# Convolution taps on ScalarE and GpSimd, two matrix-engine channel blocks, a projection four abreast, and moved waits in the head pairs

## The chip, the core and the metric

The kernel runs on one core of a Trainium2 chip. Its engines each work through their own instruction stream and meet at semaphores: TensorE (PE, matrix products into PSUM), VectorE (DVE), ScalarE (ACT), GpSimd (POOL) and SyncE (SP, which here only issues the loads of the weights).
## The reference, cut to what matters

A sequence of 512 tokens with 1024 channels passes through two networks. The first is a gated block with two recurrent heads per pair (four pairs) and an output product; the second is a Conformer convolution layer, a feed-forward layer, banded attention and a second feed-forward layer. The change touches the head pairs and the convolution:

```python
def conformer_conv(x, w_pw1, b_pw1, w_dw, b_dw, ln_g, ln_b, w_pw2, b_pw2):
    a = jax.nn.glu(x @ w_pw1 + b_pw1, axis=-1)
    y = lax.conv_general_dilated(          # depthwise: 31 taps for each channel, causal
        a, w_dw[:, None, :], window_strides=(1,), padding=((30, 0),),
        dimension_numbers=('NWC', 'WIO', 'NWC'), feature_group_count=1024) + b_dw
    y = jax.nn.silu(layernorm(y, ln_g, ln_b))
    return y @ w_pw2 + b_pw2
```

So `y[t, c]` is a sum over k = 0..30 of `w_dw[k, c] * a[t - 30 + k, c]`, then a norm over the channels of each token, then a 1024 x 1024 product.

## The kernel before

**Layout.** Channels lie on the 128 partitions in 8 blocks (KC = 8), tokens along the free axis (512). A weight matrix comes as chunks of 128 output channels. A chunk n uses slot j = n % 4 in four tiles: SP loads it into `w_raw`, ScalarE rounds it into `w_hi` (`w_high`, called ahead of use as `ahead`: `ahead` of chunk n casts chunk n + 3), GpSimd subtracts to get the rest `w_lo` (`w_low`), and only then may SP load chunk n + 4 into `w_raw`. `dense` makes a chunk's product in PSUM (`gps`, slot j) from 3 x 8 matmuls of 128 x 512: high by high, high by low, low by high, for each of 8 input blocks k. It waits for `lo_ready` (the weights) and `evicted` (the PSUM slot read out), and sets `tile_done`.

**Head pairs** (`pair`, run four times, 20 chunks each). TensorE's program is: chunks 0 to 3, the token-major chunks 4 and 5 (`dense_tokens`), chunks 6 and 7, `hgrn_levels(0)` (28 small matmuls), the token-major chunks 10 and 11, `hgrn_rest(0)`, chunk 12, scores, chunk 13, scores, `attend(0, 0)`, and so on. ScalarE copies the chunks 6 and 7 out of PSUM (`rqk`, and in four pieces with the rows exchanged `unit`) and casts the weights in between. VectorE's `decayed` (18 products and 3 scalings, most with two operands in SBUF) makes the operands of `hgrn_levels`; `near_levels` and `near_eye` collect near scores for `attend`, `causal` those of the retention heads.

**Convolution.** While TensorE makes the 16 chunks of the first pointwise product (pw1), VectorE turns two chunks into one block of the gated input `glu` and fills its time with taps: `scalar_tensor_tensor` from `glu` into a PSUM bank of `aps`, two blocks abreast. It makes the 31 taps of the blocks 0 to 4 (155). The blocks 5, 6 and 7 are TensorE's (PE_CONV = 3): for each tap a 128 x 128 diagonal matrix in a high and a low part, made by ScalarE (`diagonals`, 62 for a block), is multiplied with the shifted `glu_hi` and `glu_lo` (3 matmuls a tap, 93 a block). ScalarE copies the sums out (`conv_out`). GpSimd adds up the blocks 0 to 6 of `conv` in `total` (`hbuf[3]`); two matmuls with ones give the mean (`mean_done`). Then VectorE centres, ScalarE squares, TensorE adds the squares over the channels, ScalarE makes the reciprocal root, VectorE and ScalarE build the operands `xa_hi` and `xa_lo` of the second pointwise product (pw2).

**pw2.** Its chunk 0 is made by `dense_behind`, in which 2 matmuls follow on each block of `xa_hi` as it comes and the 8 with `xa_lo` stand at the end; the chunks 1 to 7 follow by `dense`. `residual` reads each chunk out of PSUM into `res` (VectorE), builds the next operand and the squares (ScalarE), and casts the next weights.

Every engine's order is written out by hand, so the order below is the order of the program.

## Time and profile before

| | us |
|---|---|
| median of 3 runs | 1752.26 (1751.93 to 1752.62) |
| the profiled execution, device time | 1750.22 |
| its span | 1748.4 |
| TensorE busy in the span | 1671.2 (96%) |
| VectorE, ScalarE, GpSimd busy | 809.3, 766.7, 672.1 |
| mean granted TensorE clock | 0.983 |

The busy share of TensorE includes the modelled end of each matmul, so a stretch that reads as full can still run at half the clock; the granted clock and the count of matmuls in a stretch tell that. Times of rows count from the span's start.

### The profile page before, as it was taken

Reading aid. Unit: us, or ns where it says so; the run is one execution under the profiler, and the core shown is the slowest. Engines: PE = TensorE matmul, PEld = TensorE weight load, DVE = VectorE, ACT = ScalarE, POOL = GpSimd, SP = SyncE. Lnnn points to the kernel's source line nnn. Section 1 sums busy time; section 2 is a strip of 40 time slices with the busy share of each in tenths; the row PEclk is TensorE's granted clock in tenths of the full one; section 3 lists DMA queues with packets and bytes.
Section 4 is the critical chain, followed back from the end, with each engine's and each line's share of the span. In section 5 each row is a group of like instructions: output and inputs, shape, how many; then the busy total and the mean of one; then the engine's idle time right before and its main releaser. Section 6 shows DMA issues by size and latency. Waiting matters only on the chain.

```text
span 1748.4 us, 22097 instructions
## 1 busy us (share of the span) xinstructions
PE 1671.2 (96%) x8005; PEld 1360.0 (78%) x8005; DVE 809.3 (46%) x1391; ACT 766.7 (44%) x1179; POOL 672.1 (38%) x281
## 2 busy tenths in 40 slices
PE   4899999999999999998999999999999999999997
PEld 2777877877877778875888888888887888888885
DVE  6864564564565539994322122126465321121123
ACT  4544554553553664646443222226476442222222
POOL 3343343343343434312444444445223444344342
PEclk7999999999999999998999999999999999999999
DMA  9321331331331446201223223223211333222231
GB/s 373 103 91 57 103 105 60 101 102 50 107 98 58 134 70 183 96 1 44 90 95 103 89 96 101 92 96 120 73 49 60 98 96 96 96 96 96 96 96 61
DMA packets 49876, 167.59 MB, mean 96 GB/s; under 512 B 4987, under 2 KB 9500, under 8 KB 49308
## 3 DMA queue, kind: packets, MB, share of 16 engines
q1 hardware_dynamic: 43696, 154.50, 26.6%
q10 hardware_dynamic: 6124, 12.33, 3.0%
q8 instruction: 38, 0.62, 0.2%
q14 instruction: 18, 0.15, 0.0%
HBM read 161.56 MB, written 5.24 MB: 95 GB/s over the span
## 4 chain that ended last, share of the span: by engine, by line
PE 83%; DVE 8%; ACT 4%; issue 3%; POOL 1%; DMA 0%; ACTq 0%; DVEq 0%; POOLq 0%
PE gps L1379 23%; PE gps L1381 23%; PE gps L1380 22%; POOL w_lo L431 1%; DVE ada_w L910 1%; PE gps L1408 1%; PE gps L1630 1%; PE gps L1632 1%; PE gps L1631 1%; PE gps L1409 1%; PE gps L1410 1%; PE aps L1548 1%; PE aps L1682 1%; DVE at_near L1005 1%; DVE gates L1125 1%
## 5 line engine op out<-in xcount | busy, mean ns | idle before, releaser
L431 POOL TENSOR_TENSOR w_lo<-w_raw,w_hi 128x1024 fp32r<-128x1024 f32 x260 | 644.8, 2483 | 980.6 <-ACT w_hi L495 980.6
L1379 PE MATMUL gps<-xa_hi,w_hi 128*128 128x512 f32 x1152 | 460.3, 400 | 21.2 <-POOL xa_lo L438 13.3
L1381 PE MATMUL gps<-xa_hi,w_lo 128*128 128x512 f32 x1152 | 450.5, 391 | 0.0
L1380 PE MATMUL gps<-xa_lo,w_hi 128*128 128x512 f32 x1152 | 450.3, 391 | 0.0
L495 ACT CAST w_hi<-w_raw 128x1024 fp32r<-128x1024 f32 x260 | 270.9, 1045 | 154.4 <-PE gps L1381 137.0
L1379 PE MATMUL gps<-xb_hi,w_hi 128*128 128x512 f32 x736 | 291.6, 396 | 2.4 <-issue 1.2
L1381 PE MATMUL gps<-xb_hi,w_lo 128*128 128x512 f32 x736 | 288.9, 393 | 0.0
L1380 PE MATMUL gps<-xb_lo,w_hi 128*128 128x512 f32 x736 | 286.3, 389 | 0.0
L1379 PEld LDWEIGHTS gps<-xa_hi,w_hi 128*128 128x128 f32 x1152 | 217.5, 189 | 74.9 <-issue 18.5
L1380 PEld LDWEIGHTS gps<-xa_lo,w_hi 128*128 128x128 f32 x1152 | 217.7, 189 | 46.2 <-issue 3.1
L1381 PEld LDWEIGHTS gps<-xa_hi,w_lo 128*128 128x128 f32 x1152 | 217.3, 189 | 46.0
L1379 PEld LDWEIGHTS gps<-xb_hi,w_hi 128*128 128x128 f32 x736 | 138.4, 188 | 33.0 <-issue 3.6
L1381 PEld LDWEIGHTS gps<-xb_hi,w_lo 128*128 128x128 f32 x736 | 138.2, 188 | 32.0
L1380 PEld LDWEIGHTS gps<-xb_lo,w_hi 128*128 128x128 f32 x736 | 138.2, 188 | 31.1 <-issue 0.5
L1284 DVE TENSOR_TENSOR hbuf<-gps,rstd 128x512 f32<-128x512 f32 x44 | 30.4, 692 | 202.1 <-PE gps L1381 202.1
L1227 DVE SCALAR_TENSOR_TENSOR aps<-glu,vec,aps 128x512 f32<-128x512 f32 x145 | 99.6, 756 | 1.0
L1408 PE MATMUL gps<-w_hi,xa_hi 128*128 128x256 f32 x256 | 75.4, 295 | 14.5 <-POOL w_lo L431 14.5
L1296 DVE TENSOR_TENSOR res<-gps,res 128x512 f32 x32 | 22.1, 692 | 143.8 <-PE gps L1381 143.8
L1283 DVE TENSOR_TENSOR sq<-gps,rstd 128x512 f32<-128x512 f32 x44 | 30.4, 692 | 121.4 <-PE gps L1381 106.2
L782 ACT ACTIVATE sq<-sq 128x512 f32<-128x512 f32 x44 | 27.9, 634 | 118.4 <-DVE sq L1283 118.4
L1409 PE MATMUL gps<-w_hi,xa_lo 128*128 128x256 f32 x256 | 74.9, 293 | 0.0
L1410 PE MATMUL gps<-w_lo,xa_hi 128*128 128x256 f32 x256 | 74.8, 292 | 0.0
(252 smaller groups left out, 1955.0 us busy)
## 6 DMA issues: line engine op xcount, KB each, us to landing
w_raw<-weights_dram SPq DMA_DIRECT2D x268, 512.0 KB, 3.3
ada_w<-ada_in_dram SPq DMA_DIRECT2D x8, 1024.0 KB, 15.8
gates<-ret_tab_dram ACTq DMA_DIRECT2D x4, 1024.0 KB, 5.8
rel_scratch_dram<-rel_rows ACTq DMA_DIRECT2D x1, 3072.0 KB, 34.5
x<-x_turned_dram SPq DMA_DIRECT2D x2, 1024.0 KB, 9.7
res<-xT_dram ACTq DMA_DIRECT2D x1, 2048.0 KB, 8.8
bias<-rel_scratch_dram ACTq DMA_DIRECT2D x1, 2048.0 KB, 8.5
outT_dram<-y SPq DMA_DIRECT2D x8, 256.0 KB, 2.2
```

What stands on the lines that cost most here:

```text
L431: TT(w_lo[:, j, :], w_raw[:, j, :], w_hi[:, j, :].bitcast(F32), ALU.subtract).then_inc(lo_ready[j], 1)
L495: nc.scalar.copy(w_hi[:, j, :], w_raw[:, j, :]).then_inc(hi_ready[j], 1)
L782: nc.scalar.activation(sq[:, m, :], sq[:, m, :], ACT.Silu).then_inc(silu_ready, 1)
L1227: made_at[c] = own.mark(STT(bank, src, w, bank, ALU.mult, ALU.add))
L1283: TT(sq[:, m, :], full(I, 2 * m), rstd[:], ALU.mult).then_inc(evicted[2 * m], 1)
L1284: TT(h, full(I, 2 * m + 1), rstd[:], ALU.mult).then_inc(evicted[2 * m + 1], 1)
L1379: mm(gps[:, j, :], w_hi[:, j, w], x[0][:, k, :], start=k == 0, stop=False)
L1380: mm(gps[:, j, :], w_hi[:, j, w], x[1][:, k, :], start=False, stop=False)
L1381: last = mm(gps[:, j, :], w_lo[:, j, w], x[0][:, k, :], start=False, stop=k == blocks - 1)
L1408: mm(out, x[0][:, k, tok], wh, start=k == 0, stop=False)
L1409: mm(out, x[1][:, k, tok], wh, start=False, stop=False)
L1410: last = mm(out, x[0][:, k, tok], wl, start=False, stop=k == KC - 1)
```

## The change

In words:

- **Taps.** VectorE makes the blocks 0, 2 (its taps 0 to 19 only), 3, 4 and 5: 144 taps, three blocks abreast at the end, in three banks of `aps`, by the plan of `tap_schedule`. Block 1 and the taps 20 to 30 of block 2 (42 in all) are made by ScalarE as products into five buffers (the first of them straight into `conv`) and added into `conv` by GpSimd (41 adds, each waiting for the one before it). TensorE makes only the blocks 6 and 7.
- **Mean.** GpSimd adds only the blocks 0 and 1; the others enter the mean by six matmuls with ones, three within the last block's taps, four with the last one behind them.
- **Diagonals.** Those of the second TensorE block are made one by one, with three products after every fourth.
- **pw2.** `dense_abreast` makes the chunks 0 to 3 together: for each block k of `xa_hi` 8 matmuls (two for each chunk), then the parts with `xa_lo` chunk by chunk. The cast of chunk 3 is moved ahead. The eight `normed_residual` of VectorE move from before the mean to behind the centring (four) and behind the building of the operands (four). The reciprocal root stands in `lnv`.
- **Pairs.** For the chunks 6 and 7 ScalarE casts the next weights first, frees the PSUM slot after one copy, and makes `unit` from `rqk` in SBUF. TensorE makes k = 6, 7 of chunk 13 behind the scores of the retention heads. VectorE runs `near_eye(1)` ahead of a product and a gate.

The new schedule and the core of the diff:

```python
def tap_schedule():
    stop = {c: SHARED_AT if c == SHARED_CHUNK else TAPS for c in DVE_CHUNKS}
    ...
            c = min(bank, key=lambda c: last[c])
            run.append((c, done[c], bank[c], done[c] == stop[c] - 1))
            done[c] += 1
            last[c] = n
            n += 1
            if done[c] == stop[c]:
                free.append(bank.pop(c))
                order.append(c)
```

```diff
-DVE_CONV = 5
-PE_CONV = KC - DVE_CONV
-TAP_RUNS = (8, 11, 12, 12, 12, 12, 12)
+DVE_CHUNKS = (0, 2, 3, 4, 5)
+POOL_CHUNK = 1
+SHARED_CHUNK = 2
+SHARED_AT = 20
+PE_FIRST = 6
+PE_CONV = KC - PE_FIRST
+POOL_TAPS_FROM = 10
+TAP_BANKS = (0, 2, 3)
+TAP_RUNS = (8, 10, 12, 12, 12, 12, 12)
...
             pool.wait_ge(both_ready, 1)
+            for n in range(3, 2 * KC):
+                w_low(START["pw1"] + n // SLOTS, n % SLOTS)
+                if n >= POOL_TAPS_FROM:
+                    taps(2 * (n - POOL_TAPS_FROM), 2 * (n - POOL_TAPS_FROM) + 2)
             low(0)
...
+                c, k = POOL_TAPS[i]
+                pool.wait_ge(product, i + 1)
+                if i > 1:
+                    pool.wait_ge(tap_added, i - 1)
...
+                TT(conv[:, c, :], conv[:, c, :], products[(i - 1) % len(products)], ALU.add).then_inc(tap_added, 1)
...
+                        if i > len(products):
+                            act.wait_ge(tap_added, i - len(products))
+                        nc.scalar.mul(products[(i - 1) % len(products)], src, w).then_inc(product, 1)
...
                     b = full(at(6 + n), 2 + n)
-                    nc.scalar.copy(rqk[:, n, :], b)
+                    ahead(at(7 + n), (7 + n) % SLOTS)
+                    nc.scalar.copy(rqk[:, n, :], b).then_inc(evicted[2 + n], 1)
+                    act.wait_ge(evicted[2 + n], at(6 + n) + 2)
                     for r in range(0, P, ROT_HALF):
                         o = r ^ ROT_HALF
-                        last = nc.scalar.copy(unit[o:o + ROT_HALF, n, :], b[r:r + ROT_HALF, :])
-                    last.then_inc(evicted[2 + n], 1)
-                    ahead(at(7 + n), (7 + n) % SLOTS)
+                        last = nc.scalar.copy(unit[o:o + ROT_HALF, n, :], rqk[r:r + ROT_HALF, n, :])
+                    last.then_inc(turn_ready, 1)
...
+            for k in range(TAPS):
+                diagonal(1, k)
+                if k % 4 == 3:
+                    tap_products(at, at + 3)
+                    at += 3
+                if k == 3 * TAP_GROUP - 1:
+                    conv_out(0)
+            tap_products(at, len(POOL_TAPS))
...
-                feature(13)
+                feature(13, 0, 6)
                 ret_scores(2)
                 ret_scores(3)
+                feature(13, 6)
                 attend(0, 0)
...
                 was_evicted(16)
+                near_eye(1)
                 take_norm(0, 1)
                 z_gate(17, 1, 1, "ret_norm_g")
-                near_eye(1)
...
-            for c in range(KC):
-                normed_residual(c)
...
+            for c in range(KC // 2):
+                normed_residual(c)
             dve.wait_ge(center_done, KC)
             dve.wait_ge(x_ready, KC * X_PW2)
             x_build(conv, lambda c: vcol("ln_g", c), xa_hi, xa_lo)
+            for c in range(KC // 2, KC):
+                normed_residual(c)
...
+            for c in TAPS_END[-2:]:
+                pe.wait_ge(conv_done, TAPS_END.index(c) + 1)
+                add_to_mean(conv[:, c, :])
+            pe.wait_ge(tap_added, len(POOL_TAPS) - 1)
+            add_to_mean(conv[:, SHARED_CHUNK, :])
             pe.wait_ge(conv_copied, PE_CONV)
-            mm(aps[:, 1, :], ones[:], conv[:, KC - 1, :], start=False, stop=True).then_inc(mean_done, 1)
+            add_to_mean(conv[:, KC - 1, :], last=True).then_inc(mean_done, 1)
...
+            def dense_abreast(I, x, high, low):
...
+                for k in range(KC):
+                    high(k)
+                    w = slice(k * P, (k + 1) * P)
+                    for j in range(SLOTS):
+                        mm(gps[:, j, :], w_hi[:, j, w], x[0][:, k, :], start=k == 0, stop=False)
+                        mm(gps[:, j, :], w_lo[:, j, w], x[0][:, k, :], start=False, stop=False)
+                for j in range(SLOTS):
+                    for k in range(KC):
...
+                        last = mm(gps[:, j, :], w_hi[:, j, k * P:(k + 1) * P], x[1][:, k, :], start=False, stop=k == KC - 1)
+                    last.then_inc(tile_done[j], 1)
```

GpSimd, from the last weight parts of pw1 to pw2; before (`hbuf<-hbuf,conv` are the sums of blocks):

```order
L431 TENSOR_TENSOR w_lo<-w_raw,w_hi 128x1024 x4
L462 REGISTER_ALU
L462 COMPARE_AND_BRANCH
L457 TENSOR_TENSOR glu_lo<-glu,glu_hi 128x542
L431 TENSOR_TENSOR w_lo<-w_raw,w_hi 128x1024 x2
L457 TENSOR_TENSOR glu_lo<-glu,glu_hi 128x542
L431 TENSOR_TENSOR w_lo<-w_raw,w_hi 128x1024
L457 TENSOR_TENSOR glu_lo<-glu,glu_hi 128x542
L480 TENSOR_TENSOR hbuf<-conv 128x512
L480 TENSOR_TENSOR hbuf<-hbuf,conv 128x512 x5
L431 TENSOR_TENSOR w_lo<-w_raw,w_hi 128x1024
```

and GpSimd after the change, in the second half of the same place (`conv<-conv,hbuf` and `conv<-conv,sq` are the adds of products):

```order
L497 TENSOR_TENSOR glu_lo<-glu,glu_hi 128x542
L471 TENSOR_TENSOR w_lo<-w_raw,w_hi 128x1024
...
L471 TENSOR_TENSOR w_lo<-w_raw,w_hi 128x1024
L508 TENSOR_TENSOR conv<-conv,sq 128x512 x2
L508 TENSOR_TENSOR conv<-conv,hbuf 128x512 x3
L508 TENSOR_TENSOR conv<-conv,sq 128x512 x2
L531 TENSOR_TENSOR hbuf<-conv 128x512
L508 TENSOR_TENSOR conv<-conv,hbuf 128x512 x3
...
L471 TENSOR_TENSOR w_lo<-w_raw,w_hi 128x1024 x2
```

Five sums of blocks are gone, 41 adds of products stand between the weight parts, and the last two weight parts of pw2's first four stand behind the last add.

TensorE, from the end of the convolution into pw2; before:

```order
L1632 MATMUL gps<-glu_hi,diag_lo 128x512
L1636 MATMUL aps<-hbuf,ones 128x512
L1638 MATMUL aps<-conv,ones 128x512
L1417 MATMUL aps<-sq,ones 128x512 x8
L1391 MATMUL gps<-xa_hi,w_hi 128x512
L1392 MATMUL gps<-xa_hi,w_lo 128x512
```

and TensorE at the same place after the change, from the last block's 25th tap:

```order
L1732 MATMUL gps<-glu_hi,turn_lo 128x512
L1720 MATMUL aps<-hbuf,ones 128x512
L1720 MATMUL aps<-conv,ones 128x512 x2
L1730 MATMUL gps<-glu_hi,turn_hi 128x512
...
L1732 MATMUL gps<-glu_hi,turn_lo 128x512
L1720 MATMUL aps<-conv,ones 128x512 x4
L1513 MATMUL aps<-sq,ones 128x512 x8
L1485 MATMUL gps<-xa_hi,w_hi 128x512
L1486 MATMUL gps<-xa_hi,w_lo 128x512
```

Three matmuls of the mean stand within the taps and four behind them; before there were two, both behind.

ScalarE in a pair, at the chunks 6 and 7 (`w_hi` are the casts of the chunks 10, 11 and 12); before:

```order
L616 COPY val<-gps 128x2x256 x2
L623 COPY rqk<-gps 128x512
L626 COPY unit<-gps 32x512 x4
L493 ISA
L495 CAST w_hi<-w_raw 128x1024
L623 COPY rqk<-gps 128x512
```

and ScalarE there after the change:

```order
L669 COPY val<-gps 128x2x256 x2
L546 ISA
L548 CAST w_hi<-w_raw 128x1024
L677 COPY rqk<-gps 128x512
L681 COPY unit<-rqk 32x512 x4
L548 CAST w_hi<-w_raw 128x1024
```

Each cast stands ahead of its chunk's copies.

## Rows read from the trace of the kernel before

**Rows 1.** The page's part 1: busy time, share of the span, instructions of each engine.

```profile
PE 1671.2 (96%) x8005; PEld 1360.0 (78%) x8005; DVE 809.3 (46%) x1391; ACT 766.7 (44%) x1179; POOL 672.1 (38%) x281
```

**Rows 2.** TensorE's waits over the span: waiter, releaser, total us, times, longest.

```profile
PE gps L1408 <- POOL w_lo L431: 14.5, 4, 3.6
...
PE gps L1391 <- ACT xa_hi L768: 5.5, 1, 5.5
...
PE aps L1548 <- DVE at_near L1018: 3.1, 3, 1.1
PE aps L1536 <- DVE at_r L1032: 2.4, 4, 0.6
```

**Rows 3.** Stretches: engines' busy us (instructions), granted clock, DMA share, GB/s.

```profile
646.00:718.00 72.00, 71.70 (x312) 58.63 (x313) 63.36 (x96) 35.81 (x78) 34.98 (x16) 1.00 0.69 169
718.00:783.00 65.00, 65.00 (x280) 52.52 (x279) 64.11 (x90) 39.63 (x129) 13.39 (x9) 1.00 0.05 16
783.00:799.70 16.70, 9.85 (x22) 2.98 (x20) 7.34 (x13) 12.30 (x17) 0.00 (x0) 1.00 0.00 0
799.70:811.60 11.90, 11.80 (x25) 6.27 (x26) 8.34 (x13) 10.85 (x16) 0.95 (x1) 0.57 0.00 1
811.60:855.20 43.60, 43.60 (x194) 36.04 (x193) 14.90 (x22) 16.61 (x23) 18.26 (x8) 1.00 0.29 97
```

**Rows 4.** A tap's third matmul: duration ns min/median/max, first and last start.

```profile
L1632 PE MATMUL gps<-glu_hi,diag_lo x62: 387/396/404, 718.5 to 782.8; 128*128 128x512 f32 x62
```

**Rows 5.** The chain that ended last, at the mean: start, us, what.

```profile
783.24 0.86 PE aps L1636 x2
```

**Rows 6.** VectorE in order of time, taps to centring: start, us, instruction [idle before].

```profile
721.58 23.80 DVE L1227 SCALAR_TENSOR_TENSOR aps<-glu,vec,aps 128x512 f32<-128x512 f32 x36
...
756.73 17.38 DVE L1227 SCALAR_TENSOR_TENSOR aps<-glu,vec,aps 128x512 f32<-128x512 f32 x22
...
785.18 4.88 DVE L1266 SCALAR_TENSOR_TENSOR conv<-aps,conv 128x512 f32<-128x512 f32 x8 [1.85 <-PE aps L1638]
```

**Rows 7.** GpSimd in order of time, from 711 to 779 us.

```profile
711.56 4.80 POOL L431 TENSOR_TENSOR w_lo<-w_raw,w_hi 128x1024 fp32r<-128x1024 f32 x2
...
742.47 1.30 POOL L480 TENSOR_TENSOR hbuf<-conv 128x512 f32<-128x512 f32 x1
...
774.97 1.74 POOL L480 TENSOR_TENSOR hbuf<-hbuf,conv 128x512 f32<-128x512 f32 x1 [16.77 <-DVE conv L1229]
776.86 1.56 POOL L480 TENSOR_TENSOR hbuf<-hbuf,conv 128x512 f32<-128x512 f32 x1
```

**Rows 8.** GpSimd's slowest 128 x 512 subtractions, line 438.

```profile
L438 POOL TENSOR_TENSOR xa_lo<-hbuf,xa_hi x6: 1279/2110/2260, 28.2 to 48.9; 128x512 fp32r<-128x512 f32 x6
```

**Rows 9.** ScalarE: a 128 x 512 product with a column of `vec`.

```profile
817.89 0.73 ACT L524 ACTIVATE xb_hi<-res,vec 128x512 fp32r<-128x512 f32 x1 [3.26 <-DVE res L1184]
```

**Rows 10.** A pair, in order of time: VectorE, ScalarE, GpSimd, and two later meetings.

```profile
219.82 2.51 DVE L982 TENSOR_TENSOR packed<-packed,q 128x256 f32<-128x256 f32 x7 [1.01 <-ACT hbuf L569]
...
223.52 1.06 ACT L495 CAST w_hi<-w_raw 128x1024 fp32r<-128x1024 f32 x1
...
224.66 3.38 POOL L431 TENSOR_TENSOR w_lo<-w_raw,w_hi 128x1024 fp32r<-128x1024 f32 x1 [15.95 <-ACT w_hi L495]
...
225.86 2.26 DVE L994 TENSOR_SCALAR q_far<-q_far,hbuf 128x128 f32<-128x128 f32 x1
...
228.75 4.71 POOL L431 TENSOR_TENSOR w_lo<-w_raw,w_hi 128x1024 fp32r<-128x1024 f32 x2 [0.71 <-ACT w_hi L495]
...
263.67 5.10 POOL L431 TENSOR_TENSOR w_lo<-w_raw,w_hi 128x1024 fp32r<-128x1024 f32 x1 [5.55 <-ACT w_hi L495]
...
864.93 5.23 POOL L431 TENSOR_TENSOR w_lo<-w_raw,w_hi 128x1024 fp32r<-128x1024 f32 x2 [0.47 <-ACT w_hi L495]
```

**Rows 11.** Stretches of the first and third pair, columns as in rows 3.

```profile
96.60:103.40 6.80, 5.57 (x26) 5.60 (x27) 5.54 (x10) 0.00 (x0) 3.29 (x2) 0.50 0.58 199
...
362.80:366.20 3.40, 3.40 (x18) 3.40 (x18) 2.72 (x4) 0.00 (x0) 1.60 (x1) 0.50 0.68 190
```

More of the change, by code:

```diff
@@ L53 @@
 ADA_CHUNKS = 2 * KC
-DVE_CONV = 5
-PE_CONV = KC - DVE_CONV
-TAP_RUNS = (8, 11, 12, 12, 12, 12, 12)
+DVE_CHUNKS = (0, 2, 3, 4, 5)
[5 more added lines that the diff above has]
+POOL_TAPS_FROM = 10
+POOL_TAPS = [(POOL_CHUNK, k) for k in range(TAPS)] + [(SHARED_CHUNK, k) for k in range(SHARED_AT, TAPS)]
+TAP_BANKS = (0, 2, 3)
+TAP_RUNS = (8, 10, 12, 12, 12, 12, 12)
+def tap_schedule():
+    stop = {c: SHARED_AT if c == SHARED_CHUNK else TAPS for c in DVE_CHUNKS}
+    done, bank, last, order, runs, n = {c: 0 for c in DVE_CHUNKS}, {}, {}, [], [], 0
+    free = list(TAP_BANKS)
+    for upto in range(1, KC + 1):
+        left = sum(stop[c] - done[c] for c in DVE_CHUNKS)
+        run = []
+        for _ in range(TAP_RUNS[upto - 1] if upto < KC else left):
+            new = [c for c in DVE_CHUNKS if c < upto and c not in bank and c not in order]
+            if new and free:
+                bank[new[0]] = free.pop(0)
+                last[new[0]] = -1
+            c = min(bank, key=lambda c: last[c])
[6 more added lines that the diff above has]
+                order.append(c)
+        runs.append(run)
+    return runs, order
+TAP_PLAN, TAPS_END = tap_schedule()
 TAP_GROUP = 8
 TAP_GROUPS = -(-TAPS // TAP_GROUP)
-XB_PAD = 240
+XB_PAD = 224
 PAIR_CHUNKS = 20
@@ L257, in program @@
         dve_own = sem("dve_own")
+        product = sem("product")
+        tap_added = sem("tap_added")
         consts_in = sem("consts_in")
@@ L460, in _, with taps @@
+            def taps(first, last):
+                for i in range(max(first, 1), last):
+                    tap(i)
             pool.wait_ge(both_ready, 1)
-            w_low(START["pw1"], 3)
-            with pool.Fori(START["pw1"] + 1, START["pw2"]) as i:
-                for j in range(SLOTS):
-                    w_low(i, j)
+            for n in range(3, 2 * KC):
+                w_low(START["pw1"] + n // SLOTS, n % SLOTS)
+                if n >= POOL_TAPS_FROM:
+                    taps(2 * (n - POOL_TAPS_FROM), 2 * (n - POOL_TAPS_FROM) + 2)
@@ L465, in _ @@
             low(0)
+            at = 2 * (2 * KC - POOL_TAPS_FROM)
+            taps(at, at + 6)
+            low(1)
             w_low(START["pw2"], 0)
+            taps(at + 6, at + 12)
             w_low(START["pw2"], 1)
-            low(1)
-            w_low(START["pw2"], 2)
-            low(2)
-            total = hbuf[:, 3, :]
-            for n, c in enumerate(range(1, KC - 1)):
-                if c < DVE_CONV:
-                    pool.wait_ge(conv_done, c + 1)
-                else:
-                    pool.wait_ge(conv_copied, c - DVE_CONV + 1)
-                if n > 0:
-                    pool.wait_ge(conv_sum, n)
-                TT(total, conv[:, 0, :] if n == 0 else total, conv[:, c, :], ALU.add).then_inc(conv_sum, 1)
+            taps(at + 12, TAPS)
@@ L481, in _ @@
+            total = hbuf[:, 3, :]
+            pool.wait_ge(tap_added, TAPS - 1)
+            pool.wait_ge(conv_done, TAPS_END.index(DVE_CHUNKS[0]) + 1)
+            TT(total, conv[:, DVE_CHUNKS[0], :], conv[:, POOL_CHUNK, :], ALU.add).then_inc(conv_sum, 1)
+            taps(TAPS, len(POOL_TAPS))
+            w_low(START["pw2"], 2)
             w_low(START["pw2"], 3)
@@ L1209, in normed_residual, with taps @@
                 STT(res[:, c, :], res[:, c, :], vcol("final_g", c), rstd[:], ALU.mult, ALU.mult).then_inc(res_ready, 1)
[L1211 to L1236 removed]
+            made_at = {}
+            def taps(plan):
+                for c, k, b, last in plan:
+                    src, w, bank = glu[:, c, k:k + T], vcol("w_dw", c + k * KC), aps[:, b, :]
+                    if k == 0:
+                        dve.wait_ge(evicted[2 * (c % 2)], START["pw1"] + c // 2 + 2)
+                        before = [n for n, d in enumerate(TAPS_END) if bank_of[d] == b and n < TAPS_END.index(c)]
+                        if before:
+                            dve.wait_ge(conv_done, before[-1] + 1)
+                        made_at[c] = own.mark(TS(bank, src, w, vcol("b_dw", c), ALU.mult, ALU.add))
+                    else:
+                        own.wait(made_at[c])
+                        if not last:
+                            made_at[c] = own.mark(STT(bank, src, w, bank, ALU.mult, ALU.add))
+                        else:
+                            STT(conv[:, c, :], src, w, bank, ALU.mult, ALU.add).then_inc(conv_done, 1)
+            bank_of = {c: b for run in TAP_PLAN for c, _, b, _ in run}
             def halves_in(c):
@@ L1620, in _, with add_to_mean @@
             layer_then("pw1", KC // 2, xb, x_wait(X_CONV_IN), lambda: sum_running(RMS_FIRST, double=True))
+            def add_to_mean(src, first=False, last=False):
+                return mm(aps[:, 1, :], ones[:], src, start=first, stop=last)
             for m in range(PE_CONV):
```

116 lines of the change are left out of this document (61 added, 55 removed).

## The prediction

> **What bounds the kernel.** First the busy shares: TensorE is busy for 96% of the span, every other engine for under half [rows 1]. Then its waits, which name the places where it is not: 14.5 us for GpSimd's `w_lo` in the four pairs, 5.5 at pw2, 3.1 and 2.4 in the pairs behind `near_eye` and `causal` [rows 2]. Then the stretches, with clock and counts of matmuls [rows 3]. From 646 to 783 us TensorE is full: pw1, then the taps. From 783 to 799.7 only the norm's chain runs. From 799.7 to 811.6 TensorE reads as full, but makes 25 matmuls in 11.9 us, at a mean clock of 0.57, where the next stretch makes 194 in 43.6. So what counts is TensorE's own work and the few places where it is fed too slowly. A matmul of 128 x 512 costs 43.6 / 192 = 0.227 us (8 chunks of 24), one of the taps (782.8 - 718.5) / 276 = 0.233 (the third matmul of the first and of the last of 93 taps) [rows 4].
>
> **Taps, TensorE's side.** 93 matmuls go: 93 x 0.233 = 21.7 us. The taps end at 718.0 + 186 x 0.233 = 761.3 instead of 783.0. Against that the mean grows from two ones-matmuls to seven, each 0.86 [rows 5]. Three of them stand within the taps: 764.0, plus about 0.5 for the last group of diagonals (below): 764.5.
>
> **Taps, VectorE's side.** 144 taps instead of 155. Of these 78 lie in pw1's gaps (79 before), which TensorE bounds. 66 are left from about 721.1 (one tap less stands ahead of 721.58). Two blocks abreast cost 23.80 / 36 = 0.661 a tap, one alone 17.38 / 22 = 0.79 [rows 6]. By the plan only the last 7 stand alone: 59 x 0.661 + 7 x 0.79 = 44.5, so the last `conv_done` comes at 765.6. VectorE had ended its taps at 774.9 (756.73 + 17.38 and one more) and then run `normed_residual` under TensorE's last block; both leave the path.
>
> **Taps, GpSimd's side.** An add of 128 x 512 took 1.30 alone; chained ones start 0.15 behind the end of the one before (774.97 + 1.74 = 776.71, next at 776.86) [rows 7]. So a step costs 1.45. In pw1, for each 10.9 us of TensorE (two chunks), GpSimd gets 4 adds and 2 `w_lo` of 2.40: 10.6 us. That fits, since the weights run some 5 us ahead. `low(0)` waits for ScalarE's cast behind pw1's chunk 14, which ends one chunk (5.4) ahead of the taps' start at 717.9, at 712.5; with cast, copy and subtraction (2.8) it ends at 715.3, 2.7 ahead of the taps. From there: one `glu_lo` (1.15), two `w_lo` (4.8), 30 adds and the sum of two blocks: 715.3 + 5.95 + 31 x 1.45 = 766.2. This is a tie with VectorE's 765.6. VectorE's taps read PSUM and one SBUF operand, and they kept 0.661 under the add at 742.47, which took 1.30; so I charge neither for the other. The step is the least certain term: 1.30 is its lower bound; above it stand 776.86 - 774.97 = 1.89, beside VectorE's two-operand `normed_residual`, and the slowest subtraction of this size, 2.26 [rows 8], again beside VectorE work with two SBUF operands. I take 1.45, since the adds beside taps ran alone.
>
> **ScalarE.** It was busy for 39.6 of 65 us in the taps' stretch, 124 of its 129 instructions diagonals [rows 3]. 62 of those go (18 us) and 24 products at most 0.73 each come [rows 9]: still under 45 of 49 us. But a product waits for the add five places back. The last three ahead of diagonal 28 need add 33, which is 23 steps behind 715.3 + 5.95, at 754.6; a product and six diagonals of 0.29 later, at 757.0, the group stands, and TensorE wants them at 756.5. That is the 0.5 above.
>
> **The mean.** TensorE ends at 764.5, block 5 comes at 765.6, its ones-matmul to 766.5, block 2 (add 41 at 766.2) to 767.4, block 7 to 768.3. Centring starts at 768.4 instead of 785.18 [rows 6]. **Gain 16.7 us.** The chain behind it is unchanged (four `normed_residual`, 2.6 us, fit into VectorE's wait for the root; the other four end before chunk 0 of pw2 does).
>
> **pw2.** Chunk 0 takes 11.9 us where 24 x 0.227 = 5.4 would do: 6.4 lost. `xa_hi` comes every 1.2 us, with 2 matmuls behind it; now 8, which is 1.8 us at the high clock. So feeding stops being a limit and only the clock is left. Mean 0.57 over 11.9 us means some 10.2 us at half clock [rows 3]. In the pairs, where matmuls followed back to back, a low stretch lasted 3.4 us in two of them and 6.8 in the first [rows 11]. Bounds 0 and 10.2; I take 5, nearer to rows 11 since TensorE will be as full there; it costs 2.6. Chunk 4 must wait for a read-out, a cast and a `w_lo` behind chunk 0: with chunk 0 ending 5.5 us before the four are done, 0.7 + 1.2 + 1.05 + 2.4 leaves 0.2 to wait. **Gain 6.4 - 2.8 = 3.6 us** (1 to 6).
>
> **Pairs.** (a) The 3.6 us wait for chunk 11's weights. Chunk 10's cast moves from 223.5 to 220.6 and chunk 11's from 227.6 to 224.7. But GpSimd's `w_lo` of chunk 10, free to start at 224.66, took 3.38 instead of 2.4, and at 263.67 another took 5.10: both times VectorE was in the row of 18 products of `decayed` (0.35 each for the first 14, two SBUF operands each). The first time the row went from 219.82 to 225.8; the scaling behind it then took 2.26, and GpSimd's `w_lo` ended with it at 228.04, 2.3 behind the row [rows 10]. GpSimd gets in only when the row ends. With the cast at 220.6 the row has begun, so `w_lo` of chunk 10 still ends at 228.0. Only chunk 11's moves: from 228.75 to about 228.3 (one or two of VectorE's instructions go between, as at 864.93, where two took 5.23). Gain 0.4 (bounds 0 and 2.9, rival 2; a loss only if VectorE's delay reached TensorE). VectorE then stands up to 2.4 longer before `near_levels(0)`, and with it the rotation of `rqk`; TensorE wants those only behind chunk 12, after the token chunks (12 us) and a chunk of 5.4.
> The Trainium skill (SBUF — State Buffer, "Who interferes with whom") has this as a rule: a VectorE instruction with two SBUF inputs and a GpSimd one that reads SBUF share a port pair that is held for the whole instruction. By that rule the moved cast brings little, which the 5.10 us bear out; without it the gain would be the rival's.
> (b) The 0.6 wait behind `causal`: six matmuls now stand over it, 1.4 us. Gain 0.6. (c) The 1.0 wait for `near_eye(1)`: two VectorE instructions (0.7 each) go from ahead of it. Gain 1.0. Both moved gates are wanted later than that. Four pairs: **gain 4 x 2.0 = 8.0 us.** The low stretches of the pairs (6.8, 3.4 and 3.4 us) [rows 11] I leave as they are.
>
> **Sum.** 16.7 + 3.6 + 8.0 = 28.3 us. The profiled execution goes from 1750.2 to 1721.9; the median lies 2.0 above it before, so 1752.3 - 28.3 = **1724.0 us**.
>
> **Rivals.**
> 1. GpSimd sets the end of the taps. For it: the tie above, 41 chained steps. Against: adds beside taps took 1.30. It decides from a step of 1.46. At 1.70 its last add comes at 773.9 and the mean 7.3 later: 1731.3. Chance 0.12.
> 2. `w_lo` of chunk 10 slips between VectorE's products. For it: nothing in the rows. Against: the 5.10 us. Then chunk 11's weights are there at 228.2, 2.9 us earlier than before, 2.5 more a pair; and the shorter idle may keep the clock up (13.6 us low, 6.8 lost). 1724 - 10 - 6.8 = 1707. Chance 0.08.
> 3. **Slower.** GpSimd's steps cost what its slowest subtractions did: 2.26 [rows 8] plus 0.15 = 2.41. Then the 11 adds in pw1 come 10.6 late (4.9 of it free), the 31 behind them 29.8: last add at 801.7, mean at 803.9, 18.7 later than before, against 11.6 gained elsewhere: 1752.3 + 7.1 = 1759. It decides from a step of 2.24. Against: those rows ran beside VectorE's two-operand work, the taps are not that. Chance 0.03.
> 4. The change does not do what it says at pw2 and in the pairs: TensorE stays at half clock for 10 us, the reordered waits come back elsewhere. Only the taps pay: 1752.3 - 16.7 - 1.5 = 1734. Chance 0.12.
>
> **Numbers.** The forecast has the rest, 0.65, with its own range 1718 to 1729. The range of 8 in 10 takes in rivals 1 and most of 4: 1712 to 1734. A run can tell about 0.2% (3.5 us) from no change: faster by more 0.95, within 0.02, slower 0.03.
>
> **What would show it.** TensorE's taps x186, ending at 761 of the old times (some 8 us less by the pairs' gain). Seven ones-matmuls of 0.86. The last VectorE tap and the last GpSimd add within 1 us of each other, about 44.5 and 51 us behind the last gate and `low(0)`. GpSimd's add at 1.30 with 0.15 between. Centring 16.7 earlier against pw1's end. Pairs: TensorE's wait for `w_lo` at 3.2 instead of 3.6 each, the 0.6 and 1.0 gone; GpSimd's first `w_lo` stretched to some 6 us. pw2: 96 matmuls in about 25 us, a low clock stretch of 3 to 7 us. I am wrong if GpSimd's adds take over 1.5 a step, if a new wait for `diag_ready` or a product shows on TensorE, or if the pairs change by more than 3 us each.

## The result and the profile after the change

| | before | after |
|---|---|---|
| median | 1752.11 us (4 runs, 1751.93 to 1752.62) | 1710.89 us (4 runs, 1709.66 to 1713.00) |
| profiled execution, its span | 1750.22, 1748.4 | 1709.66, 1707.9 |
| mean granted TensorE clock | 0.983 (profiled execution) | 0.984 to 0.989 (all four runs) |

The ratio is 0.9766, with a 95% interval of 0.9749 to 0.9782. Of all the runs below one was slow, 7962 us of a run of e4, and no median takes it in. The forecast of 1724.0 was 13.1 us too high, and the measured time lies 1.1 us below its range. Its direction was right, and so was its largest term. Stage by stage, from the same marks in both traces:

| stage | before | after | gain | forecast |
|---|---|---|---|---|
| start to the first cast of pw1 (mostly the pairs) | 642.66 | 626.65 | 16.0 | 8.0 |
| to the first squares of the norm (pw1, taps, mean) | 143.9 | 127.55 | 16.4 | 16.7 |
| norm and pw2 | 68.6 | 64.3 | 4.3 | 3.6 |
| the rest, whose code is unchanged | 893.2 | 889.4 | 3.8 | 0 |
| sum | | | 40.5 | 28.3 |

So two stages hold nearly the whole error of these two executions, 12.2 us: the pairs, and a part of the kernel whose code the change does not touch.

**The convolution came nearly as forecast.** VectorE, GpSimd and TensorE of the kernel after, at the end of the taps (start, us, instruction; these answer to [rows 6] and [rows 7]):

```profile
705.53 29.05 DVE L1309 SCALAR_TENSOR_TENSOR aps<-glu,vec,aps 128x512 f32<-128x512 f32 x44
...
744.38 4.70 DVE L1309 SCALAR_TENSOR_TENSOR aps<-glu,vec,aps 128x512 f32<-128x512 f32 x6
744.84 2.72 POOL L508 TENSOR_TENSOR conv<-conv,sq 128x512 f32<-128x512 f32 x2
...
747.71 1.27 POOL L508 TENSOR_TENSOR conv<-conv,hbuf 128x512 f32<-128x512 f32 x1
...
749.11 0.75 DVE L1311 SCALAR_TENSOR_TENSOR conv<-glu,vec,aps 128x512 f32<-128x512 f32 x1
...
749.91 2.84 PE L1720 MATMUL aps<-conv,ones 128*128 128x512 f32 x6 [1.18 <-DVE conv L1311]
```

A VectorE tap takes 29.05 / 44 = 0.660 (forecast 0.661). Two adds of GpSimd take 2.72, and a chained one costs 1.43 (1.45). VectorE's last tap ends at 749.86, GpSimd's last add at 748.98: the tie. A ones-matmul leaves two rows in these views (`x6` above are three of them, `x2` in [rows 5] is one), so each costs 0.86, as forecast.

**The waits of TensorE** in the kernel after (waiter, releaser, total us, times, longest), against [rows 2]:

```profile
PE gps L1504 <- POOL w_lo L471: 5.8, 4, 2.8
PE gps L1485 <- ACT xa_hi L851: 5.5, 1, 5.5
...
PE aps L1572 <- DVE packed L1068: 3.7, 6, 0.7
...
PE aps L1720 <- DVE conv L1311: 1.2, 1, 1.2
```

The wait for `w_lo` fell from 14.5 to 5.8, not to the forecast 12.8. Those for `at_near` and `at_r` are gone. One for `packed` is new.

**The pairs went in two ways.** Second pair and third pair of the kernel after, in order of time (the place of [rows 10]):

```profile
215.14 2.51 DVE L1065 TENSOR_TENSOR packed<-packed,q 128x256 f32<-128x256 f32 x7 [1.02 <-ACT hbuf L622]
...
216.99 11.03 POOL L471 TENSOR_TENSOR w_lo<-w_raw,w_hi 128x1024 fp32r<-128x1024 f32 x3 [12.96 <-ACT w_hi L548]
...
221.19 2.27 DVE L1077 TENSOR_SCALAR q_far<-q_far,hbuf 128x128 f32<-128x128 f32 x1
...
225.93 0.35 PE L1504 MATMUL gps<-w_hi,xa_hi 128*128 128x256 f32 x1 [2.85 <-POOL w_lo L471]
...
343.40 4.72 DVE L1065 TENSOR_TENSOR packed<-packed,q 128x256 f32<-128x256 f32 x7 [1.02 <-ACT hbuf L622]
345.26 2.51 POOL L471 TENSOR_TENSOR w_lo<-w_raw,w_hi 128x1024 fp32r<-128x1024 f32 x1 [12.97 <-ACT w_hi L548]
...
348.94 1.15 PE L1572 MATMUL aps<-packed 128*128 128x128 f32 x8 [0.73 <-DVE packed L1068]
```

In the second pair VectorE's row of products is undisturbed (2.51) and GpSimd waits: its three `w_lo` take 11.03 instead of some 7.2, and the first alone 6.38 instead of 2.5. In the third GpSimd gets in between two products, its `w_lo` takes 2.51, and VectorE's row takes 4.72. Both times GpSimd asks 1.85 us behind the row's start. The forecast knew the first way only. For TensorE both ways come to the same: it starts chunk 10 28.5 us behind chunk 4 in either (29.3 before).

**The low-clock stretches of the pairs are gone** in this execution: those of [rows 11] and one more, 13.6 us together. **pw2** has 3.4 us of low clock instead of 10.2. After the change, from the first to the last of the four abreast, then the rest (columns as in [rows 3]):

```profile
764.70:785.00 20.30, 17.64 (x71) 14.49 (x72) 13.12 (x20) 12.38 (x18) 0.00 (x0) 0.92 0.01 1
785.00:818.50 33.50, 33.35 (x147) 27.31 (x146) 21.56 (x22) 16.46 (x23) 18.42 (x7) 1.00 0.33 110
```

**The unchanged code got faster.** Stretches of 84 us in the feed-forward layer, TensorE full at clock 1.00; before:

```profile
856.00:940.00 84.00, 84.00 (x367) 68.60 (x366) 22.36 (x30) 37.84 (x42) 39.00 (x16) 1.00 0.29 94
```

and after:

```profile
820.00:904.00 84.00, 84.00 (x372) 69.50 (x371) 23.09 (x31) 38.30 (x43) 38.73 (x16) 1.00 0.30 99
```

367 matmuls against 372 (the records have gaps of a few, so the spacing of neighbours is the better measure: 228.9 ns against 226.7). The slower ones read `xb_hi` or `xb_lo`; those that read `xa` start every 226.7 to 226.9 ns in both kernels. The one edit that moves `xb` is `XB_PAD = 224` instead of 240: it is the size, in floats for each partition, of an unused tile ahead of `xb`. It is in the diff, and neither the words on the change nor the prediction mention it.

### The profile page after: what moved, and what is told of

Same layout as the page of the kernel before. It is cut to its first block, busy times and chain, and to the rows that moved or that the text cites. A ratio compares the mean times of both kernels' runs of the same rounds, so it can differ in the third digit from the quotient of the medians.

```text
span 1707.9 us, 21958 instructions
## 1 busy us (share of the span) xinstructions
PE 1640.8 (96%) x7922; PEld 1339.2 (78%) x7922; DVE 821.4 (48%) x1380; ACT 773.1 (45%) x1157; POOL 734.0 (43%) x316
## 4 chain that ended last, share of the span: by engine, by line
PE 79%; DVE 11%; ACT 3%; issue 3%; POOL 2%; DMA 1%; ACTq 0%; DVEq 0%; POOLq 0%; SPq 0%
PE gps L1458 22%; PE gps L1460 22%; PE gps L1459 22%; DVE aps L1309 4%; POOL w_lo L471 2%; DVE ada_w L993 1%; PE gps L1504 1%; PE gps L1506 1%; PE gps L1505 1%; DMA w_raw<-weights_dram 1%; PE aps L1644 1%; PE aps L1792 1%; PE aps L1572 1%; PE aps L1650 1%; PE aps L1802 1%
## 5 line engine op out<-in xcount | busy, mean ns | idle before, releaser
L471 POOL TENSOR_TENSOR w_lo<-w_raw,w_hi 128x1024 fp32r<-128x1024 f32 x260 | 662.4, 2551 | 923.8 <-ACT w_hi L548 923.7
L1458 PE MATMUL gps<-xa_hi,w_hi 128*128 128x512 f32 x1128 | 452.2, 401 | 21.0 <-POOL xa_lo L478 13.0
L1460 PE MATMUL gps<-xa_hi,w_lo 128*128 128x512 f32 x1128 | 441.5, 391 | 0.0
L1459 PE MATMUL gps<-xa_lo,w_hi 128*128 128x512 f32 x1128 | 441.5, 391 | 0.0
L1458 PEld LDWEIGHTS gps<-xa_hi,w_hi 128*128 128x128 f32 x1128 | 213.2, 189 | 74.3 <-issue 18.8
L1459 PEld LDWEIGHTS gps<-xa_lo,w_hi 128*128 128x128 f32 x1128 | 213.5, 189 | 45.0 <-issue 3.1
L1460 PEld LDWEIGHTS gps<-xa_hi,w_lo 128*128 128x128 f32 x1128 | 213.1, 189 | 45.4
L1309 DVE SCALAR_TENSOR_TENSOR aps<-glu,vec,aps 128x512 f32<-128x512 f32 x134 | 91.5, 745 | 0.7
```

The lines of the kernel that those rows point to most:

```text
L471: TT(w_lo[:, j, :], w_raw[:, j, :], w_hi[:, j, :].bitcast(F32), ALU.subtract).then_inc(lo_ready[j], 1)
L1309: made_at[c] = own.mark(STT(bank, src, w, bank, ALU.mult, ALU.add))
L1458: mm(gps[:, j, :], w_hi[:, j, w], x[0][:, k, :], start=k == 0, stop=False)
L1459: mm(gps[:, j, :], w_hi[:, j, w], x[1][:, k, :], start=False, stop=False)
L1460: last = mm(gps[:, j, :], w_lo[:, j, w], x[0][:, k, :], start=False, stop=k == blocks - 1)
```

## The experiments

All times are medians. The changed kernel itself is 1710.9, and 1711.6 when run again beside some of these (e5); the kernel before is 1750.5 to 1752.1, by chip. A run's low-clock stretches move it by 1 to 3 us, so differences under 2 us are read from the traces, not from the medians.

### The place of xb: 240, 224 and others

```diff
-XB_PAD = 224
+XB_PAD = 240
```

> The changed kernel with XB_PAD back at 240, so xb_hi and xb_lo lie 64 bytes further on, nothing else. In the stretches whose code the change leaves alone, matmuls that read xb started every 226.7 ns after the change and every 228.9 ns before it; those that read xa 226.7 in both. Theory (placement): the 2.2 ns come from where xb lies. Then all 2208 xb matmuls (3 x 736) start every 228.9 ns again, and the time rises by 2208 x 2.2 ns = 4.9 us, to about 1715.8. Rival (something else in the change, or the state of the chip in that execution): 226.7 ns stays and the time stays within 1.5 us of 1710.9.

Measured 1716.5 (1714.4 to 1719.1), 5.2 above the mean of the changed kernel's two medians. The spacing is 229 ns again.

> The kernel before with XB_PAD = 224 and nothing else. Placement: its xb matmuls start every 226.7 ns, the time falls by 4.9 us, from 1752.1 to 1747.2. Rival: 228.9 ns and 1752 stay. If placement is right, both this and the run on the changed kernel must move, by the same 4.9 with opposite signs.

Measured 1746.7, ratio 0.9977 (0.9966 to 0.9987), 4.3 faster; spacing 226.7. **Both directions moved by about what 2208 matmuls at 2.2 ns give, 4.9.** The traces say it without the noise of the low stretches. From the first matmul with `xb_hi` behind pw2 to the end the kernel before takes 898.9 us and the changed one with 240 takes 898.5; all 14 profiled executions with 224, that of e2 among them, take 894.9 to 895.4. pw1 takes 93.1 with 240 and 92.4 to 92.5 with 224. Placement is shown as the cause. The pad also moves every tile behind `xb`, `glu` among them; but matmuls that read `xa` and the taps, which read `glu`, keep their spacing, so it is the place of `xb` that counts. What about it counts took four more runs, each with another number in the same line:

> The changed kernel with XB_PAD = 232: xb_hi and xb_lo lie 32 bytes further on than at 224 and 32 short of 240. At 224 their matmuls start every 226.7 ns, at 240 mostly every 228.9. If any distance from the good place costs the same: 228.9 ns, 1715.8. If the cost grows with the distance: more or less than that. If only the place at 240 is bad: 226.7 ns, 1711.

> The changed kernel with XB_PAD = 192: xb lies 128 bytes ahead of its place at 224. By the allocation its byte address in a partition is 118912 at 224, a multiple of 128, 64 past one at 240 (228.x ns) and 32 past one at 232 (229 to 233 ns, 13 us slower). If the 128-byte alignment counts: 226.7 ns and 1711. If the place itself counts (distance to w_hi or another tile): another spacing, more than 228 ns.

> The changed kernel with XB_PAD = 160, so xb lies 256 bytes ahead of its good place (byte 118656 of a partition). The good place, 118912, differs from the places of w_hi, w_lo and xa_hi (32896, 49280, 65664) by multiples of 2048; those at +64, +32 and -128 bytes do not and were slow. If what counts is a distance to these tiles that is a multiple of 256, this one is good: 226.7 ns, 1711. If only a larger multiple counts, it is slow like 192: 229 to 233 ns, 1723 to 1726.

> The changed kernel with XB_PAD = 96, 512 bytes ahead of the good place. Multiple of 512 (or of 256): 226.7 ns, 1711. If only 1024 or 2048 counts: slow, 1716 to 1726.

| pad | bytes from the place at 224 | spacing in the feed-forward layer, ns | median, us |
|---|---|---|---|
| 240 | +64 | 228.9 | 1716.5 |
| 232 | +32 | 233.3 | 1723.9 |
| 192 | -128 | 232.4 to 233.3 | 1725.6 (2 runs) |
| 160 | -256 | 226.7 to 226.8 | 1712.6 (2 runs) |
| 96 | -512 | 226.7 to 226.8 | 1713.2 (2 runs) |

From the first matmul with `xb_hi` behind pw2 to the end it takes 906.7 us at pad 232, 906.0 at 192, and 895.0 at 160 and at 96. One row of each, TensorE's groups by line in a stretch of 84 us of the feed-forward layer (out<-in, count, busy us, mean ns; the mean is the length of one row, which goes with the spacing but is not the spacing); pad 232:

```profile
L1459 PE MATMUL gps<-xb_lo,w_hi 128*128 128x512 f32 x106 | 41.9, 395 | 0.0
```

and pad 160:

```profile
L1459 PE MATMUL gps<-xb_lo,w_hi 128*128 128x512 f32 x118 | 45.9, 389 | 0.0
```

Alignment to 128 bytes, which I took for the rule after e12, fell with pad 192. Places that lie a multiple of 256 bytes from the tiles of the weights and of `xa` were good, the three others bad. Whether it is the distance to the weights or the byte address itself (all good ones leave 128 when divided by 256), no run tells apart.

### The pairs' edits, together and one by one

> The changed kernel with the three edits of the head pairs undone (the casts and copies of chunks 6 and 7, chunk 13 in one piece, near_eye behind the gate). Theory: the edits give 4 x 2.3 = 9.3 us by the shorter waits, and a further 6.8 us because the long wait for the w_lo of chunk 11 (3.6 us, now 1.0 to 2.8) was what made the clock fall: low-clock stretches come back behind that wait in two or three of the pairs. Time 1710.9 + 16 = 1727. Rival: the waits come back but the low stretches were only this kernel's luck in one execution: 1720. Forecast's own number for the edits was 8.0: 1719.

The three edits taken back: 1725.8 (1725.3 to 1726.2), 14 to 15 more. TensorE's waits in this run:

```profile
PE gps L1503 <- POOL w_lo L471: 14.4, 4, 3.6
...
PE aps L1643 <- DVE at_near L1100: 3.0, 3, 1.0
PE aps L1631 <- DVE at_r L1114: 2.4, 4, 0.6
```

A pair lasts 132.4, with a low stretch of 3.4 us in three of the four. The low stretches came back with the waits.

> The changed kernel as it is, as the measure for the three runs beside it. Expected 1710.9 (1709.5 to 1713). In its profile: a pair in which GpSimd's first w_lo gets in between VectorE's products (w_lo 2.5 us, the row of products 4.7 instead of 2.5) has no low-clock stretch behind it; one in which it does not (w_lo 4.2, TensorE's wait for w_lo 2.8 instead of 1.0) has one of 3.4 us. So far 7 of 7 and 4 of 5 pairs went that way.

Measured 1711.6 (1709.2 to 1717.2). The one pair in which GpSimd did not get in had no low stretch this time, and its first `w_lo` took 6.38, not 4.2.

```diff
-                    ahead(at(7 + n), (7 + n) % SLOTS)
-                    nc.scalar.copy(rqk[:, n, :], b).then_inc(evicted[2 + n], 1)
-                    act.wait_ge(evicted[2 + n], at(6 + n) + 2)
+                    nc.scalar.copy(rqk[:, n, :], b)
...
-                        last = nc.scalar.copy(unit[o:o + ROT_HALF, n, :], rqk[r:r + ROT_HALF, n, :])
-                    last.then_inc(turn_ready, 1)
+                        last = nc.scalar.copy(unit[o:o + ROT_HALF, n, :], b[r:r + ROT_HALF, :])
+                    last.then_inc(evicted[2 + n], 1)
+                    ahead(at(7 + n), (7 + n) % SLOTS)
```

> The changed kernel with the casts of the chunks 10 and 11 behind the copies again (rqk and unit both from PSUM), the other two pair edits kept. Forecast's number for this edit: 0.4 a pair, 1.6 us in all: 1712.5. Present theory: TensorE's wait for w_lo is 3.6 in every pair again instead of 1.0 or 2.8, less the 1.2 us that it now waits for packed: 1.0 a pair (4 us), and the longer wait lets the clock fall in all four pairs, 3.4 us of it each (1.7 us of time): 1710.9 + 4 + 4 = 1719.

Measured 1721.3 (1719.9 to 1721.6): 9.7 for an edit forecast at 1.6. The pairs last 130.6, 130.3 and 131.6, where the changed kernel has 128.2. Less 1.6 for each 3.4 us of low clock (below) that is 129.0, 128.7 and 128.4: **the waits alone are worth some 0.5 a pair, near the forecast (0.4); the rest is the clock**, low in all four pairs. The 0.5 is a lower bound: two of these low stretches began while TensorE still stood, and cost less than 1.6 for each 3.4. Read at the start of chunk 10, ahead of the low stretches, the edit is worth 0.8 to 0.9 (29.3 against 28.5 behind chunk 4).

```diff
-                feature(13, 0, 6)
+                feature(13)
                 ret_scores(2)
                 ret_scores(3)
-                feature(13, 6)
```

> The changed kernel with chunk 13 in one piece ahead of the retention scores. Forecast: the 0.6 us wait for at_r comes back in each pair, 2.4 us: 1713.3. Rival: the scores then come earlier and something behind them (attend, the gates) is late by as much, so nothing changes: 1711.

Measured 1716.3, 4.7 more. Its undisturbed pairs last 128.8, so 0.6 a pair is the edit, as forecast. The one with a low stretch lasts 130.4: 1.6 for 3.4 us of low clock. That stretch (columns as in [rows 3]):

```profile
226.90:230.20 3.30, 3.30 (x18) 3.30 (x17) 2.83 (x5) 0.00 (x0) 1.16 (x1) 0.51 0.76 228
```

> The changed kernel with VectorE's near_eye(1) behind the product and the gate of chunk 17. Forecast: TensorE waits 1.0 us for at_near in each pair again, 4 us: 1714.9. The trace before had that wait three times, 3.1 us: 1714.0. Rival: nothing, 1711.

Measured 1718.2, 6.6 more. Its undisturbed pairs last 129.6 and 129.5: 1.3 for the edit (forecast 1.0). The wait for `at_near` is back at 3.1 in all.

So the waits are worth (0.5 to 0.9) + 0.6 + 1.3 = 2.4 to 2.8 a pair against 2.0 forecast; all three together 2.7 (the one pair of the kernel before without a low stretch lasts 130.9, those of the changed kernel 128.2).

### What lets the clock fall

All profiled executions but those of e9 and e13, which change TensorE's order there, can be counted together: 18 executions, 72 pairs, sorted by TensorE's longest idle time between chunk 7 and chunk 10, and by whether the clock was low in the 18 us that begin 2 us behind the start of chunk 10's `w_lo`:

| longest idle, us | pairs | with a low stretch |
|---|---|---|
| up to 1.0 (GpSimd got in among the first seven products only) | 33 | 0 |
| 2.65 to 2.9 | 23 | 18 |
| 3.6 (the old order of casts) | 16 | 13 |

The expectations of e9 quote an earlier count with 15 of 16 for the last row; it is 13. So not every long idle time was followed by a low clock, but no short one was. In the 13 executions with the changed order of casts and nothing that forces it, GpSimd failed to get in in 20 of 52 pairs, though it always asked 1.85 us behind the row's start. Nine of the 20 executions also have a low stretch of 3.4 us behind the pairs, between 563 and 590 us; what brings it is open.

```diff
                         TT(q_part, q_part, right(qe, level), ALU.mult)
+                    if e == 0:
+                        dve.wait_ge(lo_ready[2], at(10) + 2)
                     for level in range(LEVELS):
```

> The changed kernel in which VectorE waits, between the 7 products with q and the 7 with key of decayed(0), until w_lo of chunk 10 is made. So GpSimd always gets in (in the changed kernel it did in about 3 pairs of 4) and TensorE's wait for w_lo should be 1.0 in all four pairs. If the length of that idle time is what lets the clock fall: no low-clock stretch in any pair, mean clock at the upper end of the changed kernel's runs (0.988 or more in every run), 1710, with a narrower spread. If the low stretches are chance, they come in one pair of four as before and 1711.5 stays.

Measured 1715.7, 4 slower, low stretches in two pairs. The expectation missed. VectorE waits, and then the next `w_lo` gets in among the second seven products:

```profile
220.49 4.65 DVE L1070 TENSOR_TENSOR packed<-packed,key 128x256 f32<-128x256 f32 x7 [2.30 <-POOL w_lo L471]
...
221.71 2.41 POOL L471 TENSOR_TENSOR w_lo<-w_raw,w_hi 128x1024 fp32r<-128x1024 f32 x1 [1.26 <-ACT w_hi L548]
...
225.19 4.12 PE L1574 MATMUL aps<-packed 128*128 128x128 f32 x20 [2.65 <-DVE packed L1070]
```

TensorE is idle for 2.65 in one piece, now for `packed`, and the clock falls: nearly the same length, another cause of the wait. The same came by itself in the third pair of e1, with a low stretch too. That speaks for the idle time as such. An order in which GpSimd gets in every time, and only once, was not found.

### Taking the wait away altogether

```diff
+                for low in range(2):
                     for t in range(NT):
...
+                            if low:
+                                last = mm(out, x[0][:, k, tok], wl, ...)
+                            else:
+                                mm(out, x[0][:, k, tok], wh, ...)
+                                mm(out, x[1][:, k, tok], wh, ...)
```

> The changed kernel with another order in dense_tokens (chunks 4, 5 and 10, 11 of a pair, and two chunks later on): first the 64 matmuls with w_hi, which wait only for the casts, then the 32 with w_lo. The w_lo then has some 7 us more. Theory: the idle time of TensorE in front of these chunks (1.0 to 2.8 us a pair, 5.8 in all) goes, and with it every low-clock stretch behind it, since these came behind 15 of 16 waits of 3.6 us, 5 of 7 of 2.8 and 0 of 16 of 1.0: no low stretch in any pair. 1711.2 - 5.8 - about 1.5 = 1704. Rival (the clock does not follow this wait): only 5.8 goes, low stretches in one pair in four stay: 1705.5, with low stretches in the pairs. Rival (the weights are late anyway): the wait moves to chunk 12: 1711.

Measured 1735.7 (1732.5 to 1736.6): 24 slower, against every theory. First pair, VectorE, GpSimd and TensorE:

```profile
109.96 5.14 POOL L471 TENSOR_TENSOR w_lo<-w_raw,w_hi 128x1024 fp32r<-128x1024 f32 x2 [10.23 <-ACT w_hi L548]
110.25 2.63 DVE L1054 TENSOR_TENSOR packed<-cum 128x256 f32<-128x256 f32 x1
112.80 2.58 DVE L1055 TENSOR_TENSOR packed<-cum 128x256 f32<-128x256 f32 x1
...
119.38 0.71 DVE L1101 COPY_PREDICATED at_near<-eye_mask,aps 128x512 f32<-128x512 int32 x1
...
120.14 3.35 PE L1616 MATMUL aps<-rqk 64*128 64x512 f32 x6 [5.20 <-DVE at_near L1101]
```

The wait for `w_lo` is gone, and TensorE comes sooner to the scores. But the casts come sooner too, so two `w_lo` fall into VectorE's subtractions of `exponents(1)` and hold up two of them (2.6 each where the others take 0.41). `near_eye(0)` behind them is 4.4 late, TensorE stands for 5.2, and each pair has 6.8 to 10.2 us of low clock:

```profile
118.80:128.80 10.00, 8.66 (x19) 5.51 (x20) 4.45 (x10) 7.98 (x7) 3.61 (x2) 0.51 0.04 9
```

In the changed kernel `near_eye(0)` ends 0.9 to 1.2 us before TensorE's scores begin. That was all the room there was.

```diff
-                dve.wait_ge(rot_ready, p * 2 + 2)
-                exponents(1)
                 near_eye(0)
+                dve.wait_ge(rot_ready, p * 2 + 2)
+                exponents(1)
```

> The changed kernel with the order of e9 in dense_tokens (parts with w_lo last) and VectorE's near_eye(0) ahead of exponents(1) instead of behind it. In e9 TensorE waited up to 5.2 us a pair for near_eye(0), which stood behind 14 products of exponents(1), and the clock then fell for 6.8 to 10.2 us in each pair. Theory: with the 14 products out of its way near_eye(0) is done 5 us ahead of its need, so neither wait is left, no low-clock stretch comes in a pair, and the gain looked for in e9 appears: 1711.2 - 5.8 - 1.5 = 1704. Rival: VectorE is simply the longer chain of a pair once TensorE's waits are gone; the wait then moves to at_r or packed and the time stays above 1711.

Measured 1711.6, but in two groups: 1708.6, 1708.7, 1708.8 and 1714.4 against 1726.9 and 1727.0. The undisturbed pairs last 127.8. In the profiled execution one pair lasted 133.4: there GpSimd got into `exponents(1)` and TensorE waited 3.1 for `at_r`. Neither theory: three runs gain 2 to 3 us, and two lose 15 to 16. Neither of these two was profiled, so what made them slower is not shown. No version beat the changed kernel in its median.

> The changed kernel with near_eye(0) ahead of exponents(1) and nothing else. In the changed kernel near_eye(0) ends 1.8 us before TensorE's scores begin, so it is covered: no change, 1711, within 2 us. If it is faster by more, a hidden wait hung on it; if it is slower, ScalarE's decays(1) (which wait for exponents(1), now 0.6 later) are tight.

Measured 1718.5 (1712.4 to 1724.2), 7 slower instead of equal. In one pair VectorE waits 2.42 for `near_eye(0)`'s input; `exponents(1)` then starts later and meets the two `w_lo`, and TensorE waits 4.2 for `at_r`. The 1.8 us of the expectation were 0.9 to 1.2, and they were room at the place where `near_eye(0)` stood, not at the place to which I moved it.

### pw2, and who ends the taps

```diff
-            dense_abreast(START["pw2"], xa, ...)
-            layer("pw2", xa, first=SLOTS)
+            dense_behind(START["pw2"], 0, xa, ...)
+            layer("pw2", xa, first=1)
```

> The changed kernel with pw2's chunk 0 made alone again as the operand comes (dense_behind) and chunks 1 to 7 after it, everything else as changed. Theory: four abreast is worth the 4.3 us that the stage became shorter, most of it by a low-clock stretch of 3.4 instead of 10.2 us: time 1715.2, with a low stretch of about 10 us at chunk 0. Rival: the shorter low stretch came from the shorter idle before it (the mean) and not from the order: the stretch stays at 3.4 us and the time rises by only 6.4 - 3.4/2 - 2.8 lost in feeding, 1 to 2 us, to 1712.5.

Measured 1715.8 (1713.6 to 1717.4), 4 to 5 more; the low stretch is 13.7 us. From the first squares to the first matmul with `xb_hi` it takes 63.9, in the changed kernel 58.7, before 63.0. The idle time before it was the same (5.5), so the shorter low stretch comes from the order. In all 17 profiled executions with the four abreast it was 3.4 or 6.8 us, in the three others 10.2 or 13.7.

```diff
-SHARED_AT = 20
+SHARED_AT = 24
```

At 24 ScalarE's loop over the products is also bounded by their number, which is 38 then.

> The changed kernel with block 2 shared at tap 24 instead of 20: VectorE makes 4 taps more (0.66 each), GpSimd 4 adds fewer (1.43 each). In the changed kernel VectorE's last tap ends at 749.9 and GpSimd's last add at 749.0. If VectorE sets the end: centring starts 4 x 0.66 = 2.6 us later, 1713.8. If GpSimd sets it (first rival of the forecast): up to 5.7 us earlier, bounded by TensorE's own end at 747.7, so 1 to 2 us faster.

```profile
PE aps L1720 <- DVE conv L1311: 4.8, 1, 4.8
```

> The changed kernel with block 2 shared at tap 16: VectorE 4 taps fewer, GpSimd 4 adds more, ScalarE 4 products more. If the two really tie, GpSimd now ends 4 x 1.43 = 5.7 later, at 754.7, and sets the end: centring 4.8 us later, 1716. Together with the run at 24: if both are slower by their own engine's step, the forecast's tie is shown. If the step of GpSimd grows beside VectorE (forecast's 1.89 or 2.41), the loss is 7.6 or more.

```profile
PE aps L1720 <- POOL conv L508: 5.1, 1, 5.1
```

Measured 1720.6 and 1719.6, 8 to 9 more each. At 24 TensorE waits for VectorE, whose last tap ends 3.2 later against the start of TensorE's taps than at 20. At 16 it waits for GpSimd, whose last add ends 5.6 later, for four adds of 1.43: **both were at the limit, the tie is shown**. Both lose more than their own engine's step: behind a wait of 5 us the clock is low, so that each of the two rows of a ones-matmul takes 0.86 instead of 0.43, and the profiled execution at 24 also had three pairs with a low stretch.

## Why the prediction was wrong where it was

- **"The low stretches of the pairs ... I leave as they are": this step failed**, and with the place of `xb` below it is the largest part. They cost the kernel before 5.7 us in its profiled execution (two pairs of 133.6 and 132.5 against 130.9, and 1.6 for the last; half of their 13.6 us would be 6.8). The changed kernel lost none in its own, which was in part luck: one of its four pairs had the 2.85 us of idle time behind which 18 of 23 pairs had a low stretch. By the counts above a usual execution has 20/52 x 18/23 x 4 = 1.2 stretches of 1.6 us. So some 4 of the 13 us. The text had the mechanism among its rivals ("the shorter idle may keep the clock up"), and bound it to the chance of 0.08 that `w_lo` slips in. Rival 2 came true in part: the clock nearly in full, its 10 us of waits hardly. The prediction's own sign of being wrong, pairs that change by more than 3 us each, came in two of the three pairs that can be measured from start to start.
- **"GpSimd gets in only when the row ends": wrong**, in 32 of 52 pairs. What was inferred from rows of before in which GpSimd asked late (4.8 us behind the start of the first row of seven) did not hold for a request at 1.85. The gain in waits was still small, 0.5 to 0.9 a pair against 0.4, since VectorE's 2.2 us of delay came back to TensorE as the wait for `packed` (1.2).
- **The Trainium skill (SBUF — State Buffer, "Who interferes with whom")** has the lock held for the whole instruction. The traces agree: one subtraction of 0.41 becomes 2.6 when a `w_lo` of 2.4 stands before it. It says nothing of whole rows of instructions; that was my addition.
- **A line of the diff was not priced.** `XB_PAD` moved 2208 matmuls by 2.2 ns, forecast 0. By the lengths of the stages that is 4.6 us: 0.7 in pw1 and 3.9 behind pw2. The sum had a term for each stage that the change names, and took the rest as unchanged.
- **(b) and (c)**: mechanism right, 0.6 and 1.3 against 0.6 and 1.0.
- **Convolution, forecast 16.7, measured 16.4: right in its steps, but the closeness is in part luck**, since 0.7 of the 16.4 is the place of `xb`. From the start of the taps to the centring the forecast has 50.4 and the trace 51.4. TensorE's taps, GpSimd's step, the ones-matmuls of 0.86 and the tie came as forecast, and the wait for the diagonals was 0.3 to 0.4 for 0.5. The missing 1.0 is VectorE's start: it came to its last 66 taps 4.2 us behind the start of TensorE's taps, not 3.1. Rivals 1 and 3 (GpSimd's step over 1.46) did not occur.
- **pw2, forecast 3.6, measured 4.3**: the low stretch was taken as 5 us. It was 3.4 here and 6.8 in 14 of the 17 profiled executions with the four abreast. Rival 4 did not occur.

For the two profiled executions the parts add up: placement 4.6, the pairs' clock 5.7, their waits 4 x 0.7 = 2.8, pw2 0.7, less 1.0 in the convolution and 0.7 by which TensorE came later to chunk 4 of its first pair, together 12.1 of 12.2. Between the medians, where the error is 13.1, the clock's part is about 4, and some 2 us stay open.
